# Zero rows of the expert output go out half beside each attention, from SyncE in place of GpSimd

## The reference

```python
mod = silu(c) @ w_ada + b_ada                 # six rows of shift, scale and gate
h = rms_norm(x, g_pre_mix) * (1 + sc1) + sh1
proj = h @ w_in                               # 1448 columns
y_mla = mla_attention(c_q, c_kv, k_rope, ...) # 8 heads, causal
y_dsa = dsa_attention(q_d, k_d, v_d, ...)     # 8 heads over the 128 best keys of each query
mix = concatenate([y_mla, y_dsa]) @ w_o
x = x + gt1 * rms_norm(mix, g_post_mix)
h2 = rms_norm(x, g_pre_ffn) * (1 + sc2) + sh2
x = x + gt2 * rms_norm(moe_ffn(h2), g_post_ffn)  # 32 experts, the best 4 of each token
```

## Time and profile before

| | |
|---|---|
| three runs, median (lowest to highest) | 3336.52 us (3334.28 to 3943.83) |
| profiled execution, its own time | 3333.86 us |
| profiled execution, span | 3332.0 us |
| PE, DVE, ACT, POOL busy | 88%, 66%, 49%, 3% of the span |
| DMA | 660.94 MB, mean 198 GB/s |

### The profile page before, as it was taken

The page is one execution under the profiler, slowest core; times in us unless marked ns, Lnnn a source line. Parts: engine busy times, 40 slices in busy tenths (PEclk is TensorE's granted clock), DMA queues, the critical chain, the costliest instruction groups (busy, mean ns, idle before and its releaser), DMA issues. The chain is left out here.

```text
span 3332.0 us, 41278 instructions
## 1 busy us (share of the span) xinstructions
PE 2930.7 (88%) x13577; PEld 2321.5 (70%) x13577; DVE 2191.4 (66%) x3087; ACT 1619.6 (49%) x2103; POOL 113.1 (3%) x130
## 2 busy tenths in 40 slices
PE   7766792538999999999999778889999998899998
PEld 5544562437888888888888556568888775578887
DVE  6546751348999999999999666555444455554444
ACT  5322231217888888888888432433322224432332
POOL 0000020020000000000000200000000000000000
PEclk9876656759999999999999889999999999999999
DMA  9300097138999999999999731123323321132232
GB/s 356 123 19 0 7 340 262 37 127 330 390 378 392 383 384 392 382 386 390 377 392 391 271 122 57 33 79 93 101 97 100 108 69 40 52 107 82 96 101 89
DMA packets 275541, 660.94 MB, mean 198 GB/s; under 512 B 21869, under 2 KB 114301, under 8 KB 275418
## 3 DMA queue, kind: packets, MB, share of 16 engines
q1 hardware_dynamic: 245986, 549.20, 44.5%
q0 software_dynamic: 22592, 87.45, 7.2%
q10 hardware_dynamic: 6840, 22.65, 1.7%
HBM read 583.65 MB, written 75.58 MB: 198 GB/s over the span
## 5 line engine op out<-in xcount | busy, mean ns | idle before, releaser
L1194 DVE TENSOR_TENSOR weights_low<-pieces,weights_high 128x1024 fp32r<-128x1024 f32 x768 | 890.8, 1225 | 72.7 <-ACT weights_high L1187 63.4
L1187 ACT ACTIVATE weights_high<-pieces 128x1024 fp32r<-128x1024 f32 x768 | 804.4, 1061 | 202.4 <-PE banks L373 202.3
L371 PE MATMUL banks<-weights_high,xT_high 128*128 128x512 f32 x1024 | 403.5, 394 | 1.3 <-DVE weights_low L1194 1.3
L372 PE MATMUL banks<-weights_low,xT_high 128*128 128x512 f32 x1024 | 399.9, 391 | 0.0
L373 PE MATMUL banks<-weights_high,xT_low 128*128 128x512 f32 x1024 | 399.5, 390 | 0.0
L1809 ACT ACTIVATE weights_high<-pieces 128x1024 fp32r<-128x1024 f32 x192 | 200.7, 1053 | 323.2 <-DMA pieces<-in_w_up 249.8
L1813 DVE TENSOR_TENSOR weights_low<-pieces,weights_high 128x1024 fp32r<-128x1024 f32 x192 | 233.5, 1223 | 128.0 <-ACT weights_high L1809 127.3
L371 PE MATMUL banks<-hT_high,weights_high 128*128 128x512 f32 x704 | 282.4, 401 | 2.8 <-DVE hT_low L2835 2.8
L372 PE MATMUL banks<-hT_low,weights_high 128*128 128x512 f32 x704 | 274.8, 390 | 0.0
L373 PE MATMUL banks<-hT_high,weights_low 128*128 128x512 f32 x704 | 274.6, 390 | 0.0
L371 PEld LDWEIGHTS banks<-weights_high,xT_high 128*128 128x128 f32 x1024 | 193.0, 188 | 52.7 <-issue 13.5
(11 more groups left out here) (426 smaller groups left out, 4712.7 us busy)
## 6 DMA issues: line engine op xcount, KB each, us to landing
pieces<-in_w_mlp SPq DMA_DIRECT2D x768, 512.0 KB, 7.6
expert_out<-mask POOLq DMA_DIRECT2D x32, 1536.0 KB, 31.5
pieces<-in_w_up SPq DMA_DIRECT2D x64, 512.0 KB, 3.9
pieces<-in_w_down SPq DMA_DIRECT2D x64, 512.0 KB, 3.4
pieces<-in_w_in SPq DMA_DIRECT2D x56, 512.0 KB, 5.2
pieces<-in_w_ada SPq DMA_DIRECT2D x48, 512.0 KB, 7.5
expert_out<-y ACTq DMA_DIRECT2D x32, 512.0 KB, 7.6
pieces<-in_w_out SPq DMA_DIRECT2D x16, 512.0 KB, 4.3
```

The lines of the kernel that those rows point to most:

```text
L371: nc.tensor.matmul(out, a[0], b[0], start=start, stop=False)
L372: nc.tensor.matmul(out, a[0], b[1], start=False, stop=False)
L1187: self.core.nc.scalar.activation(self.hi[:, c % E_PARTS, :], self.raw[:, c % E_RAW, :], ACT.Copy).then_inc(self.high.sem, 1)
L1194: self.core.nc.vector.tensor_tensor(self.lo[:, c % E_PARTS, :], self.raw[:, c % E_RAW, :], self.hi[:, c % E_PARTS, :], ALU.subtract).then_ ...
```

## The change

`attention_stage` gives `aside` to SP in place of POOL. `zero_later_blocks` takes a range of experts. The first attention (in `mla_stages`) now gets an `aside` too and issues the zeros of experts 0 to 15; the second one issues those of experts 16 to 31. The DMAs, their sizes, the semaphore and the wait at L1307 are as they were.

```diff
         with nc.Block() as block:
             if aside is not None:
-                @block.gpsimd
-                def _(pool):
-                    aside(pool)
+                @block.sync
+                def _(sp):
+                    aside(sp)
...
-def mla_stages(core, proj, y, hT, cos, sin, W, prepare):
+def mla_stages(core, proj, y, hT, cos, sin, W, prepare, aside):
...
-        attention_stage(core, units, QK1 ** -0.5, prepare)
+        attention_stage(core, units, QK1 ** -0.5, prepare, aside=lambda sp: aside(sp, range(E // 2)))
...
-        attention_stage(core, units, HD ** -0.5, alibi, aside=aside)
+        attention_stage(core, units, HD ** -0.5, alibi, aside=lambda sp: aside(sp, range(E // 2, E)))
...
-            mla_stages(core, proj, y, hT, cos, sin, W, selection(core, sel, best))
+            mla_stages(core, proj, y, hT, cos, sin, W, selection(core, sel, best), aside)
...
-    def zero_later_blocks(self, pool):
+    def zero_later_blocks(self, sp, experts):
...
-        for e in range(E):
+        for e in experts:
...
-            pool.dma_start(later, zeros.unsqueeze(1).broadcast_to([P, rows, S - P])).then_inc(self.zeroed.sem, 16)
+            sp.dma_start(later, zeros.unsqueeze(1).broadcast_to([P, rows, S - P])).then_inc(self.zeroed.sem, 16)
```

## The result

The changed kernel runs in 3281.9 us (median of 4 runs, 3275.29 to 3284.28) against 3335.4 us for the kernel before; the ratio is 0.9848 with a 95% interval of 0.9817 to 0.988. The forecast was 3277 us, range 3266 to 3290. Single runs of either kernel now and then take far longer (3943.83 us among the four of before; 6553.06 us, and 4991.16 us for before, beside experiment 5), which the medians count and the ratios leave out. The profiled execution took 3281.6 us, its span is 3279.6 us.

What follows compares the result with a forecast made beforehand. The prediction took PE's 57.2 us idle behind the second attention, waiting for POOL's zeros to land, as the bound; 57.0 + 0 + 0 + 1.5 = 58.5 us off 3333.86 gave 3275.4, median put at 3277 us, range 3266 to 3290.

Steps and rivals of the forecast that it cites:

- The gap is POOL's stay in the block, a DMA time: Behind the second attention PE waits until POOL's zeros have landed; without POOL's part the transposes start 57.0 us earlier.
- First share beside the first attention for nothing: In the first attention, SP's 16 zero DMAs run hidden beside DVE's work; price on the path 0 us.
- 76 us for a share, 67 to 84: Time for 16 DMAs, 25.17 MB, on SP's queue beside an attention: some 76 us, between 67 and 84.
- The dear bound: Upper bound for a share on SP's queue: 194 packets a us of 1536 bytes, 298 GB/s, 84 us.
- Whether SP waits for the landing: At an attention block's end, SP might have to see its zeros land before leaving; no size given.
- all of it from the earlier start, none from SyncE: Over both attentions, the whole 57 us come from starting one half of the zeros earlier, none from the new issuer.
- The clock, +1.5 us, bounds -1.7 to +4.6: At the transposes behind the second attention, TensorE's clock stays higher without the idle gap: 1.5 us gained.
- Everything behind moves ahead as a whole: Behind the transposes, the `w_o` stage, router and experts move ahead unchanged, keeping no time of their own; no extra cost.
- the verdict "within 2%": Whole kernel: measured time within 2% of the kernel before, chance 0.89; faster by more 0.08, slower by more 0.03.
- the clock's turn over the whole of the second attention: Rival: TensorE's clock at the upper level throughout, 45 us less; half way 22 us, about 3255 us; chance 0.06.
- the slow queue: Rival: SP's zero DMAs take long and SP holds both attention blocks until landing; from 3310 us up, chance 0.04.
- a small overshoot: Rival: SP's shares run 84 to 100 us and slightly outlast the attentions; 3277 to 3290 us, chance 0.06.

Runs made afterwards that it cites:

- experiment 5: Changed kernel with SP's fills split 22 and 10, then 8 and 24, over first and second attention: 3281.39 us and 3287.83 us (8 and 24 again: 3285.72 us).
- experiment 1: Changed kernel with all 32 fills issued by SP beside the second attention, none beside the first: 3315.43 us, ratio 0.9942 to the kernel before.
- the kernel of 24 and 8: Changed kernel with 24 of SP's fills beside the first attention and 8 beside the second: 3290.0 us, ratio 0.9854 to the kernel before.
- experiment 4: Changed kernel with larger first shares from SP, 24 and 8, then 32 and 0: 3290.0 us and 3323.46 us.
- experiment 2: Changed kernel with the two shares of 16 issued by POOL in place of SP: 3278.75 us, ratio 0.9828 to the kernel before.

## Why the prediction was right, point by point

- *The gap is POOL's stay in the block, a DMA time.* Right. The gap went from 57.27 to 0.33 us, where 57.0 us were forecast. In experiment 1 SP's stay makes a gap again, and in the kernel of 24 and 8 the landing shows up at the key positions.
- *First share beside the first attention for nothing.* Right: 99.7 us long with the zeros beside it for 70 of them, DVE's busy time 88.35 us. Experiment 5 shows room for 22.
- *76 us for a share, 67 to 84.* Cheaper: 70 us. The dear bound took the packets a us of the loads as the limit. SP's queue did make one packet of each run of 1536 bytes (25.17 MB / 16640 = 1513 bytes), but moved 16640 / 70 = 238 of them a us, over the 194 that I had read from the earlier trace rows. The conversion was right and the limit wrong: the bytes a us were nearly the same in both, 367 GB/s in the earlier trace rows and 360 here.
- *Whether SP waits for the landing* was left open. It doesn't (experiments 1 and 4); it is through with 16 issues about 9 us ahead of the landing. With shares of 16 this decides nothing.
- *By the rule of the Trainium skill (DMA: Bandwidth & Descriptors, section "Issuing engines are not separate DMA queues"), all of it from the earlier start, none from SyncE.* Right for this change (experiment 2: the split from POOL gives 0.9828). My conclusion that 32 from SP would give "about that of before" was wrong by 20 us: it left out that SP leaves its block ahead of the landing and that its DMAs leave no pause.
- *The clock, +1.5 us, bounds -1.7 to +4.6.* This term failed. I had taken the level at the attention's end from one trace. It is the one or the other in either kernel, and when it is low the attention is 2.7 us longer; before, POOL's gap covered that, now it is on the path. So it was 0 or about -2.7 us, and the lower bound was too high. The transposes themselves came at 5.21 us where I had hoped for 2.9. Those 2.9 were half of 5.74 us, but of the 5.74 us only a part was at the lower level (the clock was 0.78 at 568 to 572 us). The two traces with the upper level throughout them have 3.69 us, so the most to be had there was 2 us. The stretch at the lower level behind them stayed as well: the clock was 0.58 at 576 to 580 us before, and it is 0.50 at 518 to 520 us in the changed kernel.
- *Everything behind moves ahead as a whole.* Not quite. The tail grew by 5.5 us between the two profiled executions. From the transposes to ACT's last store of expert rows it is 0.5 us shorter, so up to there all did move ahead as a whole. Then come 3.1 us more up to PE's transposes of `h_rows`, by POOL's later gathers, which no step of mine had. The last 2.8 us lie behind that, within what those stages scatter by in either group of traces (1404 to 1410 us).
- The sum: 58.5 us forecast, 52.4 in the traces, 0.0152 x 3335.4 = 51 us by the ratio. The forecast was too high by the clock's term and the tail (1.5 hoped for, 2.8 and 5.5 lost, 9.8 together), and 0.5 and 3.3 us of that came back by the shorter way to the second attention and by an earlier start of the first one. The 3.3 us are luck: the start lies ahead of anything that was changed, and it moves from 294.7 to 299.8 us over the 14 traces. The measured time stayed inside the range, and the verdict "within 2%" was the likeliest.
- The rivals: the clock's turn over the whole of the second attention (worth 44 us by its own terms, 93.04 - 49, where the prediction says 45) was seen in none of the 14 traces; the slow queue was not there (4.4 us a DMA, against the 7.8 us from which it decides); a small overshoot appears only from 24 fills on, as a late load and not as a late barrier.

## What to carry to other kernels

Where a block ends with an idle stretch and full DMA engines, find the engine that issued the transfers and ask whether the barrier waits for its issue or for the landing; then count the bytes against the stretches in which the DMA engines idle, and split the work among them. Size each part by bytes over the measured rate, and keep the last landing ahead of the next load that somebody waits for at once: 22 fills of 1.5 MB fitted beside a 99.7 us stage, 24 cost 4 us of the stretch, and the same 24 beside the second attention cost nothing that can be seen, as no load followed. Once such a gap is gone, small things that it covered (here 2.7 us of clock) count.

## What the runs showed of the hardware that was not expected

- POOL holds 15 of these DMAs, takes the next only when they are all but landed, and leaves its block when its last has landed (last issue through at 556.16 us, landing at about 564.5, PE's start at 565.56; about 562 and 562.87 in the kernel before again). SP's 8, 16, 24 and 32 issues take 26.3, 60.8, 95.2 and 128.7 us, which is some 4.2 us for each one behind the eighth, and it leaves 9 to 10 us ahead of the landing. No run tells what makes POOL stay.
- The same runs of 1536 bytes go in packets of 4274 bytes from POOL and of 1513 from SP, at nearly the same rate (358 and 368 GB/s).
- POOL's first gather, over 1300 us after the zeros, came 2.3 to 3.3 us later in the kernels where POOL had lost its instructions, and not so when useless ones stood in their place. The length or the place of its instruction list would explain that; no run here tells what it is.
- A kernel without any zeros, which would give the floor, was not tried, as the gathers' tensor would then hold rows that were never written.
